# Mixture-of-experts part on one core: expert 0's weights issued first, the constants from ScalarE's queue

## The reference, cut to what matters

```python
t = h.reshape(-1, D_MODEL)                       # 256 tokens
g_idx = argmax(t @ w_rg + b_rg)                  # one of 4 groups
top_v, top_i = top_k(t @ w_re + b_re, of the group's 8 experts, 2)
combine = sum(one_hot(ids, 32) * w_sel)          # weights of the two experts of a token
for e in range(32):
    a = silu(t @ w_gate[e]) * (t @ w_up[e])      # 2048 -> 512
    y = y + combine[:, e:e+1] * (a @ w_down[e])  # 512 -> 2048
x = x + gt2 * y                                  # gt2: row 5 of the modulation
```

## Time and profile before

| what | before |
| --- | --- |
| median of 3 runs (lowest, highest) | 2360.3 us (2359.94, 2362.82) |
| span of the profiled execution | 2358.5 us |
| TensorE busy | 2203.4 us, 93% |
| VectorE busy | 1374.9 us, 58% |
| ScalarE busy | 727.3 us, 31% |
| moved by the DMA engines | 760.8 MB, 323 GB/s over the span |
| SyncE's DMA queue (q1) | 758.4 MB, 80.4% of 16 engines |
| ScalarE's DMA queue (q10) | 0.79 MB, 0.1% |
| last part (`experts`) | 1388.4 us to the end |

### The profile page before, as it was taken

How to read it: one execution, slowest core, us unless ns; L and a number is a source line. 1 busy time by engine, 2 the same in 40 slices (tenths; PEclk the granted TensorE clock), 3 DMA queues, 4 the chain that set the end, 5 groups by cost and what they waited for, 6 DMA issues and landing times. The chain is left out here.

```text
span 2358.5 us, 36100 instructions
## 1 busy us (share of the span) xinstructions
PE 2203.4 (93%) x14693; PEld 1673.4 (71%) x14693; DVE 1374.9 (58%) x2033; ACT 727.3 (31%) x1316; POOL 37.2 (2%) x62
## 2 busy tenths in 40 slices
PE   7999999999999999989999979998888888989886
PEld 6899999888999998888898755554444444444443
DVE  7768788987786898765555553333333333333334
ACT  5444444544444554466555420000000000000001
POOL 0000000000000000030000000000000000000000
PEclk9999999999999999999999989999999999999998
DMA  9778777888887787674434349999999999999996
GB/s 377 299 297 305 265 266 265 327 304 318 310 305 266 264 302 260 259 280 163 156 131 153 116 177 429 428 430 431 429 430 431 430 430 430 430 431 430 430 431 288
DMA packets 72499, 760.79 MB, mean 323 GB/s; under 512 B 8096, under 2 KB 11200, under 8 KB 13888
## 3 DMA queue, kind: packets, MB, share of 16 engines
q1 hardware_dynamic: 72240, 758.41, 80.4%
q10 hardware_dynamic: 144, 0.79, 0.1%
HBM read 756.22 MB, written 2.95 MB: 322 GB/s over the span
## 5 line engine op out<-in xcount | busy, mean ns | idle before, releaser
L1209 DVE TENSOR_TENSOR s_w_tail<-s_raw,s_w_head 128x1024 fp32r<-128x1024 f32 x292 | 343.6, 1218 | 28.4 <-ACT s_w_head L821 28.2
L997 PE MATMUL b_ps<-s_h_head,s_w_head 128*128 128x256 f32 x1184 | 342.8, 290 | 0.0
L821 ACT ACTIVATE s_w_head<-s_raw 128x1024 fp32r<-128x1024 f32 x292 | 294.4, 1051 | 147.4 <-DMA s_raw<-in_w 89.0
L999 PE MATMUL b_ps<-s_h_head,s_w_tail 128*128 128x256 f32 x1184 | 336.1, 284 | 0.0
L998 PE MATMUL b_ps<-s_h_tail,s_w_head 128*128 128x256 f32 x1184 | 336.1, 284 | 0.0
L1332 DVE SCALAR_TENSOR_TENSOR s_ada_acc<-s_raw,s_c_col,s_ada_acc 128x2048 f32<-128x2048 f32 x120 | 281.2, 2343 | 0.0
L2443 PE MATMUL b_ps<-s_raw,s_window 128*64 128x256 f32 x2048 | 231.0, 384 | 38.7 <-DMA s_raw<-in_w_up 20.7
L2443 PEld LDWEIGHTS b_ps<-s_raw,s_window 128*64 128x64 f32 x2048 | 156.9, 138 | 117.9 <-issue 33.3
L997 PEld LDWEIGHTS b_ps<-s_h_head,s_w_head 128*128 128x128 f32 x1184 | 228.2, 193 | 5.5 <-issue 5.3
L998 PEld LDWEIGHTS b_ps<-s_h_tail,s_w_head 128*128 128x128 f32 x1184 | 228.4, 193 | 0.2
L999 PEld LDWEIGHTS b_ps<-s_h_head,s_w_tail 128*128 128x128 f32 x1184 | 228.0, 193 | 0.0
(11 more groups left out here) (356 smaller groups left out, 3503.8 us busy)
## 6 DMA issues: line engine op xcount, KB each, us to landing
s_raw<-in_w SPq DMA_DIRECT2D x198, 1024.0 KB, 5.3
s_raw<-in_w_ada SPq DMA_DIRECT2D x128, 1024.0 KB, 6.5
s_raw<-in_w_gate SPq DMA_DIRECT2D x16, 4096.0 KB, 32.8
s_raw<-in_w_up SPq DMA_DIRECT2D x16, 4096.0 KB, 30.7
s_raw<-in_w_down SPq DMA_DIRECT2D x32, 2048.0 KB, 26.9
s_down<-in_w_down SPq DMA_DIRECT2D x16, 2048.0 KB, 27.4
s_spare<-in_w_gate SPq DMA_DIRECT2D x8, 4096.0 KB, 32.9
s_down<-in_w_gate SPq DMA_DIRECT2D x8, 4096.0 KB, 32.9
```

Of the source, the lines that this page charges most:

```text
L821: act.activation(w_head[:, g % SPLITS, cols], raw[:, ring, cols], ACT.Copy)\
L997: pe.matmul(out, head, m_head, start=first, stop=False, skip_group_check=True)
L999: return pe.matmul(out, tail, m_head, start=False, stop=last, skip_group_check=True)
L1209: dve.tensor_tensor(w_tail[:, g % SPLITS, cols], raw[:, slot["w", g], cols], w_head[:, g % SPLITS, cols].bitcast(F32), ALU.subtract)\
```

## The change

The three constant transfers leave SyncE's queue, so that expert 0's weights are its first issues. The table of places is issued from ScalarE's queue, behind the load of the activation table and ahead of `x_head`; the two halves of the gate's row are issued from ScalarE's queue behind `x_head` and ahead of the two Exp. Sizes, destinations, the semaphore and the wait for it at L2573 stay.

```diff
     @block.sync
     def _(sp):
-        sp.dma_start(places[:, :], d["places"]).then_inc(sem["consts"], 16)
-
-        for half_ in range(2):
-            sp.dma_start(gate_row[64 * half_:64 * half_ + 64, :, :].rearrange("p b n -> p (b n)"),
-                         mod_dram[5:6, 1024 * half_:1024 * half_ + 1024].to_broadcast([64, 1024]))\
-                .then_inc(sem["consts"], 16)
         for c in range(PIECES_E):
             load_expert_piece(sp, 0, c)
         sp.wait_ge(sem["picks"], 1)
...
+        act.dma_start(places[:, :], d["places"]).then_inc(sem["consts"], 16)
         for t in range(TT):
             act.activation(x_head[:, t, :], x[:, t, :], ACT.Copy, scale=rstd3[:, t:t + 1]).then_inc(sem["x_head"], 1)
+        for half_ in range(2):
+            act.dma_start(gate_row[64 * half_:64 * half_ + 64, :, :].rearrange("p b n -> p (b n)"),
+                          mod_dram[5:6, 1024 * half_:1024 * half_ + 1024].to_broadcast([64, 1024]))\
+                .then_inc(sem["consts"], 16)
         act.wait_ge(sem["exp_in"], 1)
```

## The result

The changed kernel takes **2377.59 us** (median of 5 runs, 2376.34 to 2378.52) against 2360.3 (5 runs): ratio 1.007, 95% interval 1.0057 to 1.0082, 17.3 us slower. Further runs of both kernels gave 2378.61 (4 runs) against 2360.76 (19 runs). The profiled execution has a span of 2376.3 us.

The account below looks back on a forecast made before the run. The expert weights stream bounds the kernel, with the gather 1.6 us behind. A 14.2 us longer wait puts the end 12.5 us later: span 2358.5 becomes 2371.0, plus 1.8 for the runs' median gives 2372.8 us, range 2364 to 2378.

Parts of the forecast that it names:

- What bounds the kernel: Last part: the weights stream sets the end once expert 1 is issued behind the gather, itself 1.6 us from being the bound.
- Gain of the earlier weights: none: SyncE's queue: expert 0's transfers move up 1.57 us, but expert 1 still waits for the gather, so no gain.
- Exp up to 1.5 us later, covered: ScalarE's queue: the added issues delay Exp and VectorE up to 1.5 us, hidden by VectorE's wait for the constants; price zero.
- One packet of each queue in turn: DMA engines: where both queues hold work, each engine alternates single packets, signals included.
- 19 turns in 22.3 us, the wait 14.2 us longer: Constants' landing: 19 turns behind weight packets, 20.1 us plus 2.2; VectorE's wait ends at 1412.3 instead of 1398.06.
- From the wait to the end: 1.6 us less: Expert 1's first packet at 1434.6 against engines otherwise turning to it at 1422.1: 12.5 us later from a 14.2 us wait.
- The sum by turns: Last part: constants' turns lengthen the wait 14.2 us; less the slack before expert 1, the end comes 12.5 us later.
- Rival B: Constants' landing: places get free turns before weights arrive, or signals take none; landing 1402 to 1409, time 2363 to 2369; chance 0.10.

Follow-up runs that it names:

- the two repaired kernels: Against the kernel before: places first on SyncE's queue, weights behind, gate halves after them or from ScalarE, awaited ahead of the expert loop; 2360.52 and 2359.89 us.
- the small rows: Changed kernel with expert 0's gate and up weights issued as four 1 MB transfers each, rows of 8 KB instead of 32 KB; 2364.16 us, ratio 1.0008.
- the second profile: The changed kernel as it stands, profiled a second time with more runs; 2378.61 us, ratio 1.0077.

## Why the prediction was right, and where its sizes were off

The forecast was 2372.8 us, by a wait that grows through packets taking turns; the measured time is 2377.6, inside the range of 2364 to 2378 by 0.4 us. That it fell inside is in part luck: it is above the 2370 to 2376 that the forecast allowed itself, and the median of the later runs, 2378.6, is above the range. Of the 4.8 us missing, 3.2 are in the last part (15.7 against 12.5); the other 1.6 are not explained by the change, and the start of the part scatters by more. By its own steps:

- **What bounds the kernel.** Right. The gather was 1.6 us from being the bound; 1.74 came back in this pair of profiles, about 1.2 on average over all.
- **Gain of the earlier weights: none.** Right: the two repaired kernels issue them 1.2 us earlier and are not faster.
- **Exp up to 1.5 us later, covered.** The cover was there and wasn't needed. I had put the gate's issues behind x_head, near 1393.5; they began during the table load, and Exp moved by nothing. The places' issue, too, didn't wait for the table. It didn't matter, as the ring held them anyway.
- **One packet of each queue in turn.** Right, and the step on which all hangs; read from four packets at the tail of one old transfer, shown by 96 against 96 here, and by the small rows, which took 14.4 us off the wait with the same bytes.
- **19 turns in 22.3 us, the wait 14.2 us longer.** Mis-sized: 17.0. Two terms, read packet by packet as averages over the 16 engines. The first weight packet on the idle engines took 2.0 us, not 1.22, and began 0.2 us later, so places' first row came 3.1 us after the part's start, where the sum has 2.2: 1.0 us. The nine turns of places then took 9.2 us, as reckoned. The gate's ten turns took 13.5 us, where the sum has 11.8: 1.7 us. A turn with a gate row took 1.6 to 1.7 us, where 1.22 + 0.19 was reckoned: 1.50 us for the weight packet in it (62 packets, 96.6% of 16 engines in 6 us), against 1.21 beside places (96 packets, 94.3% in 7.72 us). In the earlier trace rows there was no packet of 32 KB beside one of 4 KB from another queue, and I had taken the price of the one unmixed.
- **From the wait to the end: 1.6 us less.** Right within the scatter (1.74); the gather's clock added 0.56 here, which I had left out, and nothing in the second profile. The engines ran dry near 1425.5, 35 us after the part's start, and not 33: the slower turns held up expert 0 as well. It didn't matter, as expert 1 came later still.

The sum by turns with these sizes is 17.0 + 0.6 - 1.7 = 15.9, against the 15.7 of the last part. The Trainium skill's page "DMA: Bandwidth & Descriptors" speaks of whole packets of 9 to 17 descriptors drained per turn ("Queues, rings and completion order"): taken as rows of the trace, this would give bursts of nine; the 96 rows against 96 in 7.72 us, and sixteen against sixteen in a single turn (1397.0 to 1398.29), show single rows. The same page, section "Issuing engines are not separate DMA queues", says that transfers issued from several engines run on the same 16 DMA engines and interleave, and that only the time to issue is saved; here 1.57 us of issuing were saved on SyncE, and with a wait behind the interleaved transfers the part took 15.7 us more.

Rival B had some free turns through places arriving ahead of the weights. They came behind the first weight packet of each engine, which took 2.0 us, and got none; a signal did take a turn. But moved alone, with small rows ahead on the other queue, places had their free turns (4.2 us to landing).

## What to carry to other kernels

The time in which a small transfer lands, in a second queue beside a long stream, doesn't follow its bytes: on each engine it is its number of rows, signals included, times one row of the stream (19 of them, 26 us, for 0.79 MB). So put what is needed soon ahead of the stream in the same queue, or give the stream small rows; and give each small transfer a semaphore of its own, waited for at its first reader. An issue moved off a queue is worth something only if the stream behind it sets the end at that place: here a later gather did.

## What the runs showed of the hardware that I had not expected

A DMA written behind activations in ScalarE's list was issued 0.8 us before the first of them, while the table load ran (1390.96 against 1391.76). Rows of 4 KB from one queue among rows of 32 KB from another brought the engines from 433 down to 358 GB/s at full busy share, rows of 2 KB did not, and reading different rows didn't help (348). The changed kernel's first packet of 32 KB on each idle engine took 2.0 us, the next ones 1.21.
